# A mixture-of-experts layer inside a two-block transformer kernel: every second expert's V row summed by TensorE instead of VectorE

## What is computed

```
sum over the 128 chosen experts n of  gate[n] * gelu(hf . U[n]) * V[n]
```

## Time and profile before

| | us |
|---|---|
| median of the 3 runs | 3422.42 (3411.05 to 3434.35) |
| the profiled execution | 3397.89 |
| its span, from the first instruction to the last | 3396.2 |

### The profile page before, as it was taken

The page is one execution under the profiler, slowest core; times in us unless marked ns, Lnnn a source line. Parts: engine busy times, 40 slices in busy tenths (PEclk is TensorE's granted clock), DMA queues, the critical chain, the costliest instruction groups (busy, mean ns, idle before and its releaser), DMA issues.

```text
span 3396.2 us, 27414 instructions
## 1 busy us (share of the span) xinstructions
PE 2312.9 (68%) x9402; PEld 1744.6 (51%) x9402; DVE 1990.8 (59%) x4265; ACT 1033.0 (30%) x2541; POOL 756.4 (22%) x585
## 2 busy tenths in 40 slices
PE   7996888975674467776004923365787819978898
PEld 5875565764543354464004812234576318756783
DVE  1104111389878885768996699858788850631340
ACT  1003012111326642431113455435445221431220
POOL 0001000011343332330143345324322420100110
PEclk9996999987895578898557655576898958589999
DMA  5331432357998888995388987769899963002343
GB/s 212 149 137 62 161 124 95 122 219 280 355 389 344 344 342 340 354 392 223 124 333 323 355 304 268 293 242 386 347 412 394 406 238 137 1 26 99 124 152 127
DMA packets 102172, 826.42 MB, mean 243 GB/s; under 512 B 10841, under 2 KB 14185, under 8 KB 19857
## 3 DMA queue, kind: packets, MB, share of 16 engines
q0 software_dynamic: 73728, 536.90, 40.9%
q1 hardware_dynamic: 24240, 277.24, 20.8%
q10 hardware_dynamic: 4064, 10.53, 0.9%
HBM read 816.21 MB, written 8.41 MB: 243 GB/s over the span
## 4 chain that ended last, share of the span: by engine, by line
PE 40%; DVE 24%; DMA 21%; issue 7%; ACT 6%; POOL 2%; ACTq 0%; DVEq 0%; SPq 0%; POOLq 0%
PE ps L699 18%; DMA BIG<-in_uv,BIG 18%; DVE X L1615 8%; PE ps L714 7%; DVE BIG L1623 4%; PE ps L700 3%; DVE BIG L1556 2%; PE ps L928 2%; PE ps L831 1%; DVE BIG L1554 1%; PE ps L866 1%; PE ps L891 1%; ACT WK L973 1%; POOL BIG L1835 1%; PE ps L715 1%
## 5 line engine op out<-in xcount | busy, mean ns | idle before, releaser
L699 PE MATMUL ps<-BIG,RING 128*128 128x256 f32 x4704 | 1108.4, 389 | 142.8 <-ACT BIG L1018 51.6
L1835 POOL DMA_INDIRECT BIG<-in_uv,BIG x512 | 691.4, 1350 | 1745.1 <-DVE X L1615 1301.7
L699 PEld LDWEIGHTS ps<-BIG,RING 128*128 128x128 f32 x4704 | 914.7, 196 | 287.7 <-ACT BIG L1018 53.2
L1623 DVE CUSTOM_DVE_ANT_0 BIG<-BIG 128x1024 f32<-128x1024 f32 x512 | 624.6, 1220 | 177.8 <-DMA BIG<-in_uv,BIG 173.7
L1615 DVE SCALAR_TENSOR_TENSOR X<-BIG,small,X 128x1024 f32<-128x1024 f32 x512 | 655.5, 1280 | 49.6 <-ACT small L1190 49.3
L1187 ACT ACTIVATE small<-small 128x1 f32<-128x1 f32 x512 | 103.6, 202 | 1015.9 <-DVE small L1623 1014.7
L687 PE MATMUL ps<-ident,BIG 128*128 128x128 f32 x144 | 60.7, 422 | 511.2 <-ACT BIG L989 342.1
L714 PE MATMUL ps<-RING,BIG 128*128 128x512 f32 (+1 forms) x784 | 341.4, 588 | 14.8 <-DVE BIG L1398 6.2
L687 PEld LDWEIGHTS ps<-ident,BIG 128*128 128x128 f32 x144 | 32.1, 223 | 523.6 <-ACT BIG L989 349.9
L714 PEld LDWEIGHTS ps<-RING,BIG 128*128 128x128 f32 x784 | 150.6, 193 | 192.4 <-issue 175.8
L1357 DVE TENSOR_SCALAR BIG<-ps 128x256 f32<-128x256 f32 (+2 forms) x45 | 20.2, 449 | 324.1 <-PE ps L700 264.3
(11 more groups left out here) (242 smaller groups left out, 2540.5 us busy)
## 6 DMA issues: line engine op xcount, KB each, us to landing
RING<-in_w_in SPq DMA_DIRECT2D x32, 2048.0 KB, 8.7
RING<-in_w_up SPq DMA_DIRECT2D x22, 2048.0 KB, 9.0
RING<-in_w_down SPq DMA_DIRECT2D x10, 2048.0 KB, 9.8
RING<-in_w_pq SPq DMA_DIRECT2D x8, 2048.0 KB, 8.5
RING<-in_w_conv_out SPq DMA_DIRECT2D x4, 2048.0 KB, 8.5
RING<-in_w_attn_out SPq DMA_DIRECT2D x4, 2048.0 KB, 9.6
RING<-in_w_mix_out SPq DMA_DIRECT2D x4, 2048.0 KB, 10.1
RING<-in_w_ckv SPq DMA_DIRECT2D x4, 2048.0 KB, 8.0
```

What stands on the lines that cost most here:

```text
L699: e.matmul(ps[:, 0:256], W[:, j, m * 128:(m + 1) * 128], src[:, j, 0:256], start=j == 0, stop=False)
L1623: e.tensor_tensor_reduce(out=u, in0=HF[t // 2][:, t % 2, :], in1=u, scale=1.0, scalar=0.0, op0=ALU.mult, op1=ALU.add, accum_out=dots[:, k ...
L1835: e.indirect_dma_start(out=slot[i], out_offset=None, in_=I["uv"], in_offset=bass.IndirectOffsetOnAxis(ap=IDX[:, t, c:c + 1], axis=0)).then ...
```

## The change

Odd experts (`by_pe`) no longer pass DVE's sum. ACT makes one more step for them: it multiplies the identity matrix by the column of the expert (`DIAG`, 128x128, four buffers, two of them in a new tile DG), which gives a diagonal matrix of factors. PE multiplies this diagonal with the V half in two matmuls of 128x512, into PSUM banks 6 and 7, and accumulates there over the 64 odd experts of a token tile. At the end of a tile DVE adds the two banks to x (`total`, two instructions of 128x512). The even experts stay with DVE, with the sum still behind the next dot.

The slot of an odd expert is free only when PE has done its two matmuls. Its place in PE's order is in the plan: behind the steps of the plan that stand ahead of expert k + 3.

Three more things come with it. During the woven part the other work of PE has 6 banks in rotation (`("banks", 6)`). In PE's step of nsa the logits now come behind the transposes and the product with V, for both halves. The planned cost of an expert is 2.75 us (tiles 0 and 1) and 2.38 us (tiles 2 and 3), which shifts all other work against the experts.

```diff
+def by_pe(k):
+
+    return k % 2 == 1
...
     def peers(self):
+        late = []
         for t in range(4):
             while t not in self.chosen or (t == 2 and "x1" not in self.reached):
                 yield "wait"
             for c in range(128):
-                yield (3.3 if t < 2 else 2.35), "expert", t, c
-            if t == 1:
-                yield 0, "last", 255
-                self.reached.add("peer0")
-        yield 0, "last", 511
+                k = 128 * t + c
+                yield 0, "expert", t, c
+                if late and not by_pe(late[-1]):
+                    yield 0, "add", late.pop()
+                late.append(k)
+                if len(late) > 2:
+                    yield 0, "add", late.pop(0)
+                if c == 4 and t % 2:
+                    yield 0, "total", t - 1
+                yield (2.75 if t < 2 else 2.38), "pace"
+            if t % 2:
+                for k in late:
+                    yield 0, "add", k
+                late = []
+                yield 0, "total", t
+                self.reached.add(f"peer{t // 2}")
 
     def steps(self):
         yield from (s[1:] for s in self.first_a())
+        yield ("banks", 6)
         yield from weave(self.work(), self.peers(), self.choices())
+        yield ("banks", 8)
         yield from (s[1:] for s in self.second(1, False))
...
+        DIAG = [DG[:, 0, :], DG[:, 1, :], BIG[:, 32512:32640], BIG[:, 32640:32768]]
...
+            turn, held, n_banks = [0], {}, [8]
 
             def bank(*name):
-                b = turn[0] % 8
+                b = turn[0] % n_banks[0]
...
             def nsa(h, i):
                 units = nsa_units(h)
                 ncmp = cmp_n(h)[1]
-                u = i
-                if u < 16:
-                    qb, r, g = units[u]
-                    nk = (qb + 1) * 128
-                    pr = slice(64 * g, 64 * g + 64)
-                    q = QN[pr, r, (qb % 2) * 128:(qb % 2 + 1) * 128]
-                    for j, (K, nn) in enumerate(((KN[pr, 2, 0:nk], nk), (KN[pr, 3, 0:nk], nk), (KC[pr, 0:ncmp], ncmp))):
-                        ps = bank("nl", h, u, j)
-                        for m in (2, 3):
-                            w.wait_ge(*at["ev", "qn", h, 0, m])
-                            w.wait_ge(*at["ev", "kn", h, 0, m])
-                        for gg in range(2):
-                            w.wait_ge(*at["ev", "kc", h, gg])
-                        e.matmul(ps[:, 0:nn], q, K, start=True, stop=True).then_inc(pe.sem, pe("mm", "nl", h, u, j))
                 u = i - 3
...
                              start=False, stop=True).then_inc(pe.sem, pe("mm", "nv", h, u))
+                u = i
+                if u < 16:
...
+            def rotate(n):
+                n_banks[0] = n
+
+            def add(k):
+                t, c = k // 128, k % 128
+                if k == 1:
+                    for b in (6, 7):
+                        w.wait_ge(*at[("ev",) + held[b]])
+                        held[b] = ("experts", b)
+                if by_pe(k):
+                    if c == 1 and t:
+                        w.wait_ge(*at["total", t - 1])
+                    w.wait_ge(*at["gate", k])
+                    v, d = slot[k % NS][:, 1024:2048], DIAG[k // 2 % 4]
+                    e.matmul(banks[6][:, :], d, v[:, 0:512], start=c == 1, stop=c == 127)
+                    e.matmul(banks[7][:, :], d, v[:, 512:1024], start=c == 1, stop=c == 127).then_inc(pacc.sem, pacc("sum", k))
...
                 w.wait_ge(*at["gw", t])
-                e.activation(a, a, ACT.Copy, scale=GS[:, t, c:c + 1]).then_inc(gate.sem, gate("gate", k))
+                if by_pe(k):
+                    e.activation(a, a, ACT.Copy, scale=GS[:, t, c:c + 1]).then_inc(act.sem, act("gated", k))
+                    own()
+                    if k >= 8:
+                        w.wait_ge(*at["sum", k - 8])
+                    w.wait_ge(*at["ident"])
+                    e.activation(DIAG[k // 2 % 4], ident[:, :], ACT.Copy, scale=a).then_inc(gate.sem, gate("gate", k))
+                else:
+                    e.activation(a, a, ACT.Copy, scale=GS[:, t, c:c + 1]).then_inc(gate.sem, gate("gate", k))
...
-            def add_expert(k):
+            def add(k):
                 t = k // 128
+                if by_pe(k):
+                    return
                 if k == 0:
                     w.wait_ge(*at["ev", "co", 0, 1, 1])
                 elif k == 256:
                     w.wait_ge(*at["ev", "co", 1, 1, 1])
                 w.wait_ge(*at["gate", k])
-                if k % 128:
-                    w.wait_ge(*at["sum", k - 1])
+                w.wait_ge(acc.sem, acc.n)
...
-                if k not in (0, 256):
-                    add_expert(k - 1)
+
+            def total(t):
+                w.wait_ge(*at["sum", 128 * t + 127])
+                w.wait_ge(acc.sem, acc.n)
+                for hh in range(2):
+                    d = X[:, t, hh * 512:(hh + 1) * 512]
+                    e.tensor_tensor(d, banks[6 + hh][:, :], d, ALU.add).then_inc(dve.sem, dve("total", t))
+                    at["ev", "experts", 6 + hh] = (dve.sem, dve.n)
```

More of the change, by code:

```diff
@@ L440, in program @@
         pe, act, dve, pool = (Signal(sem(n), at) for n in ("pe_group", "act_result", "dve_result", "pool_result"))
-        dot, gate, acc = (Signal(sem(n), at) for n in ("expert_dot", "expert_gate", "expert_sum"))
+        dot, gate, acc, pacc = (Signal(sem(n), at) for n in ("expert_dot", "expert_gate", "expert_sum", "expert_pe_sum"))
         ring = [Signal(sem(f"ring{i}_full"), at, 16) for i in range(2)]
@@ L449, in program @@
                   for n in ("ebias", "bias", "heads_k", "heads_v0", "heads_v1", "kv", "out")}
-        signals = ([pe, act, dve, pool, dot, gate, acc] + ring + slot_in + hb_in + list(loads.values())
+        signals = ([pe, act, dve, pool, dot, gate, acc, pacc] + ring + slot_in + hb_in + list(loads.values())
                    + list(stored.values()))
@@ L898, in nsa @@
                              start=False, stop=True).then_inc(pe.sem, pe("mm", "nv", h, u))
+                u = i
+                if u < 16:
+                    qb, r, g = units[u]
+                    nk = (qb + 1) * 128
+                    pr = slice(64 * g, 64 * g + 64)
+                    q = QN[pr, r, (qb % 2) * 128:(qb % 2 + 1) * 128]
+                    for j, (K, nn) in enumerate(((KN[pr, 2, 0:nk], nk), (KN[pr, 3, 0:nk], nk), (KC[pr, 0:ncmp], ncmp))):
+                        ps = bank("nl", h, u, j)
+                        for m in (2, 3):
+                            w.wait_ge(*at["ev", "qn", h, 0, m])
+                            w.wait_ge(*at["ev", "kn", h, 0, m])
+                        for gg in range(2):
+                            w.wait_ge(*at["ev", "kc", h, gg])
+                        e.matmul(ps[:, 0:nn], q, K, start=True, stop=True).then_inc(pe.sem, pe("mm", "nl", h, u, j))
             def gmlp(h):
@@ L939, in tensor_program @@
                     "scores": scores, "cmp1": cmp1, "cmp2": cmp2, "nsa": nsa, "gmlp": gmlp, "conv_out": conv_out,
-                    "down": down, "mark": marks(pe, "pe")})
+                    "down": down, "add": add, "banks": rotate, "mark": marks(pe, "pe")})
         def norm_start(key):
@@ L958, in final_start @@
             if tag == "fa":
-                return [("sum", 255 if h == 0 else 511), ("idx", 3)] + ([("out", 0, 0), ("out", 0, 1)] if h else []) + [
+                return [("total", 1 if h == 0 else 3), ("idx", 3)] + ([("out", 0, 0), ("out", 0, 1)] if h else []) + [
                     ("mark", ("s2", h), q) for q in ENGINES]
@@ L1786, in vector_program @@
                     "da_norm": da_norm, "cross": cross, "gain": gain, "scores": scores, "top": top, "cand": cand, "pick": pick,
-                    "gates": gates, "expert": expert, "last": add_expert,
+                    "gates": gates, "expert": expert, "add": add, "total": total,
                     "final1": lambda h: final("fa", h, 16, half(h), "fin1"),
```

2 lines of the change are left out of this document (1 added, 1 removed).

## The result

| | us |
|---|---|
| kernel before, median of 4 runs | 3416.74 (3405.23 to 3434.35) |
| changed kernel, median of 4 runs | 3581.75 (3564.47 to 3591.32) |
| ratio | 1.0473 (95% interval 1.041 to 1.0536) |

The change costs 4.7% (165 us between the medians), where a gain of 59 us was forecast. The profiled execution of the changed kernel has a span of 3578.5 us against 3396.2.

A forecast was written before the change was run, and what follows sets the result against it. DMA and DVE were taken to bound the woven part by turns. 77 us gained through expert 265 and 18 us lost after it make 59 us, set against the median: 3363 us, range 3285 to 3465.

The forecast's parts named there:

- two limits that change places: Woven part: DMA share 0.90 to 0.98 in five of ten stretches, DVE over 84% busy in six.
- the hold of an odd slot: Gather slots of odd experts: held about 6 us, like even ones; 4.2 us if PE stands there already.
- The loop of the prediction: Five gather slots, in attention and nsa: (0.3 + 1.4 + 8.4 + 6) / 5 = 3.2 us for an expert.
- The first term: Slot loop in attention and nsa: 0.3 us from a free slot to its gather's issue.
- PE comes late: In projections, output projections, second block to nsa, "up" and "down": odd slots held 12 us; 3463 us; chance 0.22.
- its two signs: Woven part: gather waits mostly for line 970 (PE) instead of 1662; an expert of "up" costs over 3.9 us.
- six banks: PE's other work in the woven part: six PSUM banks cost almost nothing; another 51.6 us in projections would give 3415.
- ACT's diagonal: ACT's 128x128 step for each odd expert: 0.3 us, bounds 0.2 and 0.5, 77 us in all, costing only latency.
- "Down" behind the last expert: End of the woven part: 16 matmuls at 0.86 us, 14 us on top, now stand behind the last expert.
- the new order of nsa: Nsa of half 1: only its order changes, counted as 0, bounds -2 and +10 us.
- The choices of tiles 2 and 3: Top-k choices with 24 experts instead of 18: DVE needs 160 us, so the length stays 183 us.
- The DVE rival: Six stretches with DVE over 84% busy: DVE is the limit and they give back 198 us, so 3224; chance 0.11.

The follow-up runs named there:

- the hybrid: Changed kernel, but PE sums odd experts only in 0-42, 86-151, 242-265 and 299-366, behind expert k + 1 in attention and nsa: 3368.66 us, ratio 0.9823.
- the place behind k + 1: Changed kernel, but an odd expert's two matmuls stand behind PE's steps ahead of expert k + 1 instead of k + 3: 3562.83 us, ratio 1.046.
- the banks by role: Changed kernel, but half 1's first-block attention gets its six banks by role (logits four, transposes one, product with V one), not in rotation: 3546.26 us, ratio 1.032.
- the narrowed run: Changed kernel, but the two matmuls of an odd expert take 64 columns each instead of 512: 3480.51 us, ratio 1.0201.

## Why the prediction was wrong

**What bounds the kernel.** That two limits change places held. In the choices and in nsa DVE's relief did shorten things, once PE was early enough: that is the hybrid's gain. For the change as it stood it did not give the time, since the slots decided.

**The step that failed** is the hold of an odd slot: "I take 6 us, equal to the even ones, because PE waits for results in most stretches". The premise was right and the conclusion the wrong way round. PE that waits for results was taken for PE that has time and will be there when the gate comes. But PE is in order, and it waits at a place ahead of the odd expert's matmuls. Measured: 12.3 us in attention and 13.0 in nsa, of which 6.8 and 7.4 us are the finished expert's wait for PE. The loop of the prediction with the terms of the trace put in is (2.5 + 1.2 + 7.8 + (5.6 + 12.3) / 2) / 5 = 4.1 us for an expert in attention, against 4.05 measured and 3.2 taken; 7.8 us is the landing with the wait for the dot. That is an account of one trace and no test; the tests are the place behind k + 1 and the banks by role, which cut the hold and the stretch together. The first term, from a free slot to its issue, was taken as 0.3 us. It is 2.5 us (4.3 for even slots, 0.6 for odd ones), because POOL also issues in order and an even slot waits behind an odd one.

**The rival "PE comes late"** named the right mechanism and only half of the places; its 3463 us were 119 short. It put the lateness where PE is nearly full and expected attention and nsa to be spared. The output projections (389.4 us against its 369, hold 12.5) and the second block to nsa (171.1 us, hold 12.9) did come late. "Up" and "down", which it had at 361 us, took 317.6 with PE busy for 94% of it and a hold of 5.5 us, and the projections 157.4 against its 176: a full PE need not be late. Of the 221 us over forecast, 119 are in attention and nsa, where PE was busy for 51 and 60% of the time only. Of its two signs, the gather did wait mostly for line 970, while an expert of "up" cost 3.65 us and not over 3.9.

**The banks.** The prediction weighed six banks by the time that PE waited for a bank's reader and found almost nothing due. For six banks without experts on PE this held (ratio 1.0011 with DVE summing all). But it read PE's 117.9 us of waits on a maximum as waits for a result. The code has PE's logits waiting there for nothing but the bank. The Trainium skill ("Perfetto Trace Analysis", section "Matmul Optimizations") asks for all 8 banks to be used; in this case what mattered in attention was which reader the reused bank has: with banks by role the stretch fell from 267 to 235 us and the kernel by 35 us between the medians, without a seventh bank. What eight banks would have given there, no run shows.

**Smaller terms.** The prediction has ACT busy for at most half of any stretch; by the earlier trace rows it was 59% in attention (112.0 of 188.6 us). ACT's diagonal took 0.40 us instead of 0.3, within its bounds, and with it the diagonal was ready 2.2 to 3.7 us after the start of the dot, so it was not what cost. "Down" behind the last expert took 14.3 us as forecast:

```profile
2931.24 1.92 PE L970 MATMUL ps<-BIG 128*128 128x512 f32 x2
2932.94 14.31 PE L949 MATMUL ps<-RING,BIG 128*128 128x512 f32 x32
```

These are the rows of PE's timeline behind the last dot. The span behind the last dot grew by 9.7 us (651.0 against 641.3). With DVE alone under the same plan it was 639.9 us, so the new order of nsa cost nothing there, within its bounds of -2 and +10. The choices of tiles 2 and 3 (186.4 for 183) were right, and the stretch with experts alone did vanish, though experts 0 to 265 ended at 1900 us and not near 1770.

**The DVE rival** had the Trainium skill's rule of the engine with the highest occupancy ("Perfetto Trace Analysis", section "Identifying the Most-Contended Engine") behind it. DVE lost 289 us and the kernel grew, but the change put a wait on PE in place of DVE's time, so this alone is no test of the rule. The hybrid is nearer to one: the trace agrees with the rule in the choice of tile 1 and in nsa (17 and 22 us gained), and not in attention (3 us), where DVE was busy for 87% as well. Occupancy did not show the slots.

What stays open is the share of PE's place and of its volume in the stretches of projections with norms and cross attention. From the output projections to the scores the narrowed run had 371 us and DVE alone 357 where the changed kernel had 389, but the place behind k + 1 did not help (394). Its trace shows one reason: the wait for PE in the hold fell there from 7.0 to 1.2 us, but the diagonal came 6.2 us after the start of the dot instead of 3.6, and ACT waited 87 us for PE's projections (line 719) instead of 37. The two engines then wait for each other. In nsa no run changed the reuse of banks alone, so its share there is open too.

## What to carry to other kernels

When an engine that executes in order is given the step that frees a buffer, idle time of that engine is not enough: what it stands waiting for ahead of that step counts; price the buffer's hold from the engine's waits, stretch by stretch, and put the step ahead of the wait or give it to another engine there. Look at which reader each reused PSUM bank waits for before anything time-critical is queued behind it. And a total that hardly moves can hide two large stretches of opposite sign, which can then be had apart.

## What the runs showed of the hardware

- The highest rate taken from the rows of before, 389 GB/s, is not the ceiling: the projections of the hybrid ran at 413 GB/s with a DMA share of 1.00.
- With experts' matmuls in attention the granted clock there rose from 0.55 to 0.72, and in nsa from 0.50 to 0.68, though PE still stood idle for 49 and 40% of the time. The second matmul of an odd expert in attention was busy for 1.28 us in the mean (42.19 us for 33 of them), between the 0.86 us of full speed and twice that.
- The gather's issue on POOL got shorter: a mean of 1176 ns against 1350. Over the runs it goes with the number of sums that DVE takes: 1374 ns with all 512 of them under the new plan, 1268 with 412 (hybrid), 1220 with 384 (every fourth expert), 1176 with 256. What links the two was not tested.
